# The last head's attention of a hybrid layer, moved from slot 62 to slot 50 of its head, with other score banks and earlier value products

## The reference

```python
def differential_attention(q, k, v, lam, lam_init, subln_w):
    ...
    for blk in range(t // DA_QBLOCK):        # 4 blocks of 128 queries
        ...
        s = einsum(q[:, q0:q1], k[:, :q1]) * scale           # two maps m per head
        s = where(dist >= 0, s - slopes * dist, -inf)
        p = softmax(s)
        a = p[:, :, 0] - lam * p[:, :, 1]
        outs.append(einsum(a, v[:, :q1]))
    return rms_norm(o, subln_w) * (1.0 - lam_init)

def gated_delta_rule(...):
    ...
    state, o = scan(step, s0, (q, k, u, w, g, qk))    # each step needs the state of the step before
```

## Time and profile before

| | us |
|---|---|
| median of three runs | 1798.54 (1797.96 to 1800.02) |
| the profiled execution: its time | 1798.9 |
| the profiled execution: its span | 1797.1 |
| TensorE busy | 1759.1 |
| VectorE busy | 1205.6 |
| ScalarE busy | 680.4 |

### The profile page before, as it was taken

One profiled execution on the slowest core, in us unless ns is written; L12 is line 12 of the kernel. 1 busy time (PEld: TensorE's weight loads), 2 busy tenths in 40 slices (PEclk: granted clock), 3 DMA queues, 4 the chain that ended last, 5 costly groups with the idle time before them and its releaser, 6 DMA issues.

```text
span 1797.1 us, 28140 instructions
## 1 busy us (share of the span) xinstructions
PE 1759.1 (98%) x11282; PEld 1409.8 (78%) x11282; DVE 1205.6 (67%) x2388; ACT 680.4 (38%) x1505; POOL 7.2 (0%) x14
## 2 busy tenths in 40 slices
PE   7999999999999999999999999899999999999997
PEld 3668787888878787878877888688888888888887
DVE  4876677676858586865857755747777677784333
ACT  4335244343435353443535322433332333253221
POOL 0000000000000000000000000000000000000001
PEclk8999999999999999999999999999999999999999
DMA  9983333343323433233232877243333333324333
GB/s 382 367 341 137 125 106 124 118 145 108 123 107 118 147 106 124 106 117 136 106 129 103 287 240 238 96 147 141 112 124 129 130 117 112 142 83 152 117 119 105
DMA packets 56082, 268.03 MB, mean 149 GB/s; under 512 B 6280, under 2 KB 7944, under 8 KB 35728
## 3 DMA queue, kind: packets, MB, share of 16 engines
q1 hardware_dynamic: 55952, 266.23, 41.4%
HBM read 257.28 MB, written 8.93 MB: 148 GB/s over the span
## 4 chain that ended last, share of the span: by engine, by line
PE 94%; DMA 2%; DVE 2%; SPq 1%; ACT 0%; issue 0%; DVEq 0%; ACTq 0%
PE psum L698 26%; PE psum L700 25%; PE psum L699 25%; DMA ada_x<-in_ada_first 2%; PE psum L1167 1%; PE psum L737 1%; PE psum L738 1%; PE psum L739 1%; PE psum L1141 1%; PE psum L971 1%; PE psum L990 1%; PE psum L715 1%; PE psum L1152 1%; PE psum L849 1%; PE psum L870 1%; PE psum L981 1%
## 5 line engine op out<-in xcount | busy, mean ns | idle before, releaser
L698 PE MATMUL psum<-mov_hi,w_hi 128*128 128x512 f32 x1984 | 802.5, 404 | 5.4 <-DVE mov_lo L1743 4.3
L700 PE MATMUL psum<-mov_hi,w_lo 128*128 128x512 f32 x1984 | 775.7, 391 | 0.0
L699 PE MATMUL psum<-mov_lo,w_hi 128*128 128x512 f32 x1984 | 774.3, 390 | 0.0
L698 PEld LDWEIGHTS psum<-mov_hi,w_hi 128*128 128x128 f32 x1984 | 373.2, 188 | 93.2 <-issue 16.0
L700 PEld LDWEIGHTS psum<-mov_hi,w_lo 128*128 128x128 f32 x1984 | 372.9, 188 | 81.0
L699 PEld LDWEIGHTS psum<-mov_lo,w_hi 128*128 128x128 f32 x1984 | 374.1, 189 | 68.5
L1688 DVE TENSOR_TENSOR w_lo<-w_raw,w_hi 128x512 fp32r<-128x512 f32 x504 | 336.9, 686 | 102.3 <-ACT w_hi L1274 101.6
L1274 ACT ACTIVATE w_hi<-w_raw 128x512 fp32r<-128x512 f32 x504 | 291.5, 622 | 4.1 <-PE psum L700 3.6
L1704 DVE SCALAR_TENSOR_TENSOR ada_acc<-ada_t,silu_c,ada_acc 128x512 f32<-128x512 f32 x240 | 178.9, 746 | 10.8 <-DMA ada_t<-in_ada_late 3.6
L1563 ACT ACTIVATE osq<-res 128x512 f32<-128x512 f32 x28 | 17.8, 634 | 211.5 <-DVE res L2218 211.5
L1607 ACT ACTIVATE pr<-pr,st 128x128 f32<-128x128 f32 x128 | 49.8, 392 | 123.1 <-DVE st L2297 123.1
(11 more groups left out here) (365 smaller groups left out, 1731.3 us busy)
## 6 DMA issues: line engine op xcount, KB each, us to landing
w_raw<-in_w_pack SPq DMA_DIRECT2D x126, 1024.0 KB, 4.9
ada_t<-in_ada_late SPq DMA_DIRECT2D x128, 512.0 KB, 5.6
x_in<-in_ada_first SPq DMA_DIRECT2D x14, 1024.0 KB, 7.9
w_raw<-in_w_early SPq DMA_DIRECT2D x8, 896.0 KB, 9.1
ada_t<-in_ada_first SPq DMA_DIRECT2D x7, 1024.0 KB, 6.9
ada_x<-in_ada_first SPq DMA_DIRECT2D x7, 1024.0 KB, 11.0
res<-in_x_t SPq DMA_DIRECT2D x4, 1024.0 KB, 8.0
xr<-in_x_t SPq DMA_DIRECT2D x16, 256.0 KB, 3.6
```

The costliest lines, as they stand in the source:

```text
L698: mm(PJ[r], w_hi[r][:, ks], mov_hi[:, kt], start=(j == 0), stop=False)
L699: mm(PJ[r], w_hi[r][:, ks], mov_lo[:, kt], start=False, stop=False)
L700: ins = mm(PJ[r], w_lo[r][:, ks], mov_hi[:, kt], start=False, stop=(j == KC - 1))
```

## The change

The attention of the last head begins at slot 50. Counted from slot 64, the scores stand at -14, -14, -7, -3, `biased` at -13, -11, -6, -2, the exponentials at -12, -10, -5, -1, `combine` at -9, -7, -4, 0 and the turns at -6, -5, -2, 1; so only `combine(3)` and `turn(3)` are left in the tail slots. The scores of blocks 0 and 1 go into the banks `GO` and `OA` (which the scan's output and the values use later) and no longer into `SA0` and `SA1`, which the triangular inverse still uses at slots 50 to 56. The value products stand at tail slot 4 in place of 9. `sums_in`, `sums_hi` and `sums_lo` stay at tail slots 9 and 10, and the scan stays where it was. No instruction is added or taken away; the transfers are the same.

```diff
-        LAST_S, LAST_C, LAST_T = (-2, 0, 3, 4), (0, 2, 4, 6), (2, 4, 7, 8)
+        LAST_S, LAST_B, LAST_E = (-14, -14, -7, -3), (-13, -11, -6, -2), (-12, -10, -5, -1)
+        LAST_C, LAST_T = (-9, -7, -4, 0), (-6, -5, -2, 1)
...
-        SLOT_VALUES, LAST_VALUES, LAST_SUMS = 19, 9, 11
+        LAST_BANKS = ((GO, OA), (GO, OA), (SA0, SA1), (SA0, SA1))
+        SLOT_VALUES, LAST_VALUES, LAST_SUMS = 19, 4, 11
...
             def scan_b(h, c):
                 cc = slice(c * P, c * P + P)
                 pe.wait_ge(vn_ok, h * 4 + c + 1)
+                if c == 0 and h == NH0 - 1:
+                    pe.wait_ge(da_t, h * 8 + 4)
...
             def av_tokens(h):
                 pe.wait_ge(raw_in, h * 4 + 4)
                 pe.wait_ge(vt_ok, h + 1)
+                if h == NH0 - 1:
+                    pe.wait_ge(ATev_ok, h * 4 + 2)
...
             def scores(h, b):
-                if b == 0:
+                if b == 0 and h == NH0 - 1:
+                    pe.wait_ge(aqk_ok, h * 2 + 2)
+                    pe.wait_ge(gy_ok, h)
+                    pe.wait_ge(dy_ok, h)
+                elif b == 0:
                     pe.wait_ge(aqk_ok, h * 2 + 2)
                     pe.wait_ge(off_ok[3], h + 1)
-                elif b == 2 and h < NH0 - 1:
+                elif b == 2 and h == NH0 - 1:
+                    pe.wait_ge(off_ok[3], h + 1)
+                elif b == 2:
...
-                for m, dst in enumerate(DA_BANKS[b] if h < NH0 - 1 else (SA0, SA1)):
+                for m, dst in enumerate((DA_BANKS if h < NH0 - 1 else LAST_BANKS)[b]):
...
             def turn(h, b):
                 pe.wait_ge(da_a, h * 4 + b + 1)
-                if b == 0:
+                if b == 0 and h == NH0 - 1:
+                    pe.wait_ge(vt_ok, h + 1)
+                elif b == 0 or b == 2 and h == NH0 - 1:
                     pe.wait_ge(vtok_ok, h + 1)
...
+                if h == NH0 - 1:
+                    pe.wait_ge(da_t, h * 8 + 4)
                 ada_stage(h, OA)
...
+                if h == NH0 - 1:
+                    st[62] = [lambda: head_ada(h)]
+                    for b in range(TT):
+                        st.setdefault(8 * SLOTS + LAST_S[b], []).append(lambda b=b: scores(h, b))
+                        if LAST_T[b] < 0:
+                            st.setdefault(8 * SLOTS + LAST_T[b], []).append(lambda b=b: turn(h, b))
...
-                st.setdefault(LAST_VALUES + 1 if last else 20, []).append(lambda: sums_hi(h))
+                st.setdefault(LAST_SUMS - 1 if last else 20, []).append(lambda: sums_hi(h))
...
+                if h == NH0 - 1:
+                    for b in range(TT):
+                        st.setdefault(8 * SLOTS + LAST_E[b], []).append(lambda b=b: exps(h, b))
+                        if LAST_T[b] < 0:
+                            st.setdefault(8 * SLOTS + LAST_T[b], []).append(lambda b=b: turn_copy(h, b))
...
                     if h == NH0 - 1 and s == 8 * SLOTS - 1:
-                        exps(h, 0)
                         split_y(2)
                         split_y(3)
...
                     if h == NH0 - 1 and s == 8 * SLOTS - 2:
-                        biased(h, 0)
                         split_y(0)
                         split_y(1)
...
+                if h == NH0 - 1:
+                    for b in range(TT):
+                        st.setdefault(8 * SLOTS + LAST_B[b], []).append(lambda b=b: biased(h, b))
+                        if LAST_C[b] < 0:
+                            st.setdefault(8 * SLOTS + LAST_C[b], []).append(lambda b=b: combine(h, b))
```

More of the change, by code:

```diff
@@ L1023, in tail_stages @@
                     last = h == NH0 - 1
-                    if not last or b > 0:
-                        st.setdefault((LAST_S if last else DA_S)[b], []).append(lambda b=b: scores(h, b))
-                    st.setdefault((LAST_T if last else DA_T)[b], []).append(lambda b=b: turn(h, b))
+                    if not last:
+                        st.setdefault(DA_S[b], []).append(lambda b=b: scores(h, b))
+                    if not last or LAST_T[b] >= 0:
+                        st.setdefault((LAST_T if last else DA_T)[b], []).append(lambda b=b: turn(h, b))
                 if not last:
@@ L1470, in tail_stages @@
                     last = h == NH0 - 1
-                    if not last or b > 0:
-                        st.setdefault((LAST_S if last else DA_B)[b] + 1, []).append(lambda b=b: exps(h, b))
-                    if last or b > 1:
+                    if not last:
+                        st.setdefault(DA_B[b] + 1, []).append(lambda b=b: exps(h, b))
+                    if last and LAST_T[b] >= 0 or not last and b > 1:
                         st.setdefault((LAST_T if last else DA_T)[b], []).append(lambda b=b: turn_copy(h, b))
-                    elif b == 1:
+                    elif b == 1 and not last:
                         st.setdefault(DA_T[1], []).append(lambda: turn_copy_two(h))
@@ L2072, in biased @@
             def biased(h, b):
-                E, a = P * (b + 1), DA_S_AT[b] if h < NH0 - 1 else 0
+                E, a = P * (b + 1), DA_S_AT[b]
                 pb, s_ = plane(h, b)
-                for m, src in enumerate(DA_BANKS[b] if h < NH0 - 1 else (SA0, SA1)):
-                    dve.wait_ge(sc_ok, h * 8 + (4 if b == 0 and h < NH0 - 1 else 2 * b + m + 1))
+                for m, src in enumerate((DA_BANKS if h < NH0 - 1 else LAST_BANKS)[b]):
+                    dve.wait_ge(sc_ok, h * 8 + (4 if b == 0 else 2 * b + m + 1))
                     if m == 0 and (b > 1 or h == NH0 - 1 and b > 0):
@@ L2109, in tail_stages @@
                 last = h == NH0 - 1
-                for b in range(1 if last else 0, TT):
-                    st.setdefault((LAST_S if last else DA_B)[b], []).append(lambda b=b: biased(h, b))
                 if not last:
+                    for b in range(TT):
+                        st.setdefault(DA_B[b], []).append(lambda b=b: biased(h, b))
                     st[0].append(lambda: ada_finish(h, OA))
                 for b in range(TT):
-                    st.setdefault((LAST_C if last else DA_C)[b], []).append(lambda b=b: combine(h, b))
+                    if not last or LAST_C[b] >= 0:
+                        st.setdefault((LAST_C if last else DA_C)[b], []).append(lambda b=b: combine(h, b))
                 st.setdefault(25, []).append(lambda: gated(h, GO, tA, WDN, NH0, grn_ok, gy_ok))
-                st.setdefault(LAST_VALUES if last else 19, []).insert(0, lambda: sums_in(h))
-                st.setdefault(LAST_VALUES + 1 if last else 21, []).append(lambda: sums_lo(h))
+                st.setdefault(LAST_SUMS - 2 if last else 19, []).insert(0, lambda: sums_in(h))
+                st.setdefault(LAST_SUMS - 1 if last else 21, []).append(lambda: sums_lo(h))
                 st.setdefault(29, []).append(lambda: gated(h, OA, pa[1], WSUB, 0, drn_ok, dy_ok))
```

8 lines of the change are left out of this document (2 added, 6 removed).

## The result

The changed kernel takes 1801.09 us (median of 20 runs, 1798.85 to 1803.89), the kernel before beside it 1798.59 us (20 runs). The ratio is 1.0017, with a 95% interval of 1.0010 to 1.0023: slower by 2.5 us by the medians, by 1.8 to 4.1 by the interval. The forecast was 1802.2.

A forecast was written before the change was run, and what follows sets the result against it. TensorE was busy 1759.1 of 1797.1 us, waiting on a nearly full VectorE in the last head's stretch. To 1798.5 it added +0.2 for waits, +1.0 for the closing chain and +2.5 for the clock: 1802.2 us, range 1798.2 to 1804.4.

The forecast's parts named there:

- rival A: Likeliest case, chance 0.50: first wait grows, a second appears, end of the stretch gives time back, clock falls; 1802.2 us.
- the waits of before: Four TensorE waits around the last head's attention, 4.36 us idle plus 0.16 each, 5.0 us; 5.2 after the change.
- the clock: TensorE's granted clock falls to half rate behind the longer idle time ahead of `scan_a(2)`: +2.5 us, bounds 0 and 3.3.
- The wait for `S`: TensorE's idle time ahead of `scan_a(2)` grows from 2.51 to 3.80 us, `S` coming 0.66 later after `vnew(1)`.
- just fit: ScalarE's added work fits its 3.38 us idle before `vnew(1)`: 0 us taken, up to 0.5 in the range.
- The wait for `combine(3)`: New TensorE idle time between `scan_a(2)` and `turn(3)`: 1.05 us, costing 1.21.
- The closing chain: VectorE's steps to the last slots move up 1.15 us, TensorE 2.15, so +1.0 returns as waits; bounds 0 and 2.15.
- rival B: Same waits around `scan_a(2)`, but TensorE's clock stays at 1.00: not slower, 1799.7 us, chance 0.30.
- C: VectorE's relief is kept, first wait unchanged, `combine(3)` not waited for, end not binding: 2.3 us won, 1796.2, chance 0.10.
- D: `vnew(1)` late by 0.5, 2.15 given back at the end, low clock costing 3.3: +6.1 us, 1804.6, chance 0.10.
- the steps found just in time there: Moved attention steps in slots 50 to 62 are each done before needed, at no cost; otherwise at most about 1.68 us.

The follow-up runs named there:

- the filled kernel: The changed kernel with 16 unused matmuls of 512 columns put into TensorE's idle time ahead of `scan_a(2)`: 1799.2 us, and 1799.94 us measured again.
- the three executions: The changed kernel itself, profiled three times with nothing altered: median 1801.09 us, the two repeats 1803.38 and 1802.62 us as single times.
- the last experiment: Changed kernel with block 3's exponentials, combine and turn later, values of blocks 0 to 2 ahead of `scan_a(2)`, block 3's at tail slot 9: 1796.75 us.
- block 3 later: Changed kernel with block 3's exponentials at tail slot 0, `combine(3)` at 1, `turn(3)` at 3, values at 5: 1799.02 us.

## Why the prediction was right, and where it was not

The case was the one forecast as likeliest, rival A, and its mechanism holds, though one of its terms (the waits of before, below) came out near by luck. At full clock the prediction had +1.2 and the filled kernel measured +0.95; for the clock it had +2.5 and the three executions give 1.9, 2.4 and 3.0. The median moved by 2.5 us, where the sum was 3.7. The interval of the ratio, 1.8 to 4.1 us, takes in both, and the stretch of the three executions grew by 2.8, 3.2 and 3.7; so the 1.2 us that are missing cannot be told from the scatter of the runs, and no term is to be blamed for them.

**The wait for `S`.** Forecast 3.80, measured 4.11, released by `S`, behind the exponentials of `ck` and `cv` as described. The delay from `vnew` to `S` was right (0.66 forecast, 0.63 measured). The other 0.31 come from the assumption that ScalarE's three added steps ahead of `vnew(1)` "just fit"; they did not, by 0.35 us, which is inside the 0.5 kept for it.

**The wait for `combine(3)`.** Forecast 1.05, measured 1.09 where `scan_a(2)` ran at full clock, and 0.78 where it ran at half (the wait is shown shorter because the instruction ahead of it is longer). Moving the transposes away gave back 1.3 at full clock, against 1.21. What the prediction did not see is that the length of the low stretch may hang on it: 6.8 us in the four executions with this wait, 3.4 in the four without. The lows of 6.40 and 6.60 us from which it took its price are windows inside longer ones: from 49.2 to 56.1 and from 1141.5 to 1148.3 the clock was at 0.50 for 6.8 us each.

**The waits of before.** By the forecast's account the waits of the kernel before were worth 5.0 and those after 5.2, +0.2. With the measured waits this account would be 4.11 + 1.09 + 0.32 = 5.5, +0.5; yet at full clock, with the values at tail slot 9, the stretch takes 59.3, 0.2 less than before. So the 0.16 us added to each wait is too small for some waits of before: outside its idle rows the stretch has 59.54 - 4.36 = 55.18 us before and, with filler and idle rows taken out, 60.49 - 3.72 - 2.21 = 54.56 in the filled kernel, for the same matmuls (the filler is shown with 3.96 us, of which 0.24 overlap with `scan_b(1)`). That these 0.62 us lie in how closely the small products follow each other (those of the scores and of `solve`) is argued and not shown; no run settles it. Two errors of opposite sign met in this term: 0.3 us too little for the waits after the change, 0.6 to 0.7 too little for those before. They partly cancel, so that the sum of the waits (+0.2 forecast, -0.2 measured) came out so near is luck.

**The closing chain.** Forecast +1.0, measured 1.1 and 1.16 in two pairs. From `scan_b(3)` at 965.33 to the last slots at 976.20 it is 10.87 us, which is the 12.02 of before less the 1.15 worked out. The small waits forecast at some 0.5 each are 0.47 and 0.24.

**The clock.** The fall came, as by rival A, and rival B, which left it at 1.00, is out in all six profiles of kernels with a wait of 4.1 us. The price was 2.5 with bounds 0 and 3.3, and 1.9 to 3.0 was found. The low stretch began 3.5 to 4.5 us after the start of the idle time by the forecast; it began 2.7 us after the end of `scan_b(1)` in the first execution and 4.8 in the third (3.6 in the second), so the two long waits of before gave too narrow a picture. The rule cited from the Trainium skill, "TensorE: Matmul & The Clock Gate", section "HAM oscillation — how this bites in real kernels", is borne out by the filled kernel: with the gap filled, the loss is gone.

**Rivals C and D.** C, that the relief of VectorE is kept, is wrong for this order. The kernel of the last experiment is faster than before by about what C had (2.5 us, and 2.3), but not by C's way: it needs block 3 later, the values moved back and other work in the idle time. D supposed a late `vnew`, a chain that gives back all and the largest clock loss; only the first and, in one execution, most of the third came about.

No wait appeared in slots 50 to 62: the steps found just in time there did fit.

## What to carry to other kernels

When work is moved out of a busy stretch, read what it leaves behind. Here the four matmuls of `scores(1)` stood ahead of TensorE's longest wait and shortened it; with them gone, that wait grew by 1.60 us of idle time and a new one of 1.09 came behind it, against 1.85 for the three that went away. Of an idle time, ask whether TensorE's clock falls behind it (here behind 3.22 and 4.1 us), and what comes next: a second short wait there cost 1.3 us by itself and came with a low stretch twice as long. The best use of such a gap is work that is ready and must be done anyway; but most of what it gave here was the clock (1.7 of 2.1 us), and products for nothing give that back too.

## What was not expected of the hardware

- In the stretch the granted clock fell behind waits of 4.1 us (six executions) and of 3.22 us (two, each time after TensorE had resumed), and not behind 2.51 us (one profile). The length of one wait is not all that decides. In the profile of the kernel with filler the clock fell at 96.4 us for 3.4 us, far from the change, behind two waits of 0.89 and 1.37 us with eight products between them. None of the other eleven profiles has a fall within 20 us of it:

```profile
93.83 1.04 PE L717 MATMUL psum<-x_in,silu_c 128*1 128x512 f32 x8 [0.89 <-DMA x_in<-in_ada_first]
96.24 1.79 PE L717 MATMUL psum<-ada_x,silu_c 128*1 128x512 f32 x8 [1.37 <-DMA ada_x<-in_ada_first]
```

- Its low stretch took one of two lengths: 6.8 us in the four executions with a second wait close behind the first, 3.4 us in the four with steady work there. Near 1140 us, with one order and one wait of 3.77 us, it took 6.8 us in eight profiles and 3.4 in four, so the order does not fix it everywhere.
- Where it begins varies by 2 us between executions of one program (2.7 to 4.8 us behind the start of the idle time), which alone makes them differ by 1 us (lost: 1.9 to 3.0).
